# Low-rank product in four column groups, queries in two halves among the pieces of w_ada, rows turned by transposes, layers begun with half of the tokens, new instruction orders

## The reference, cut to what matters

```python
# block A, layers 0 and 1
shift, scale, gate = split(silu(c) @ w_ada + b_ada, 3)      # and the same for c_ctx
h  = x * (1 + scale) + shift;   hc = ctx * (1 + scale_c) + shift_c
# 16 projections of h and hc: q, k, v, gates, gla q, k, v, the low-rank pair g_af, g_ab
# (16 + 16 columns), sgu u, v, gate, and three merge gates
z = (pa @ a2 + ab)                                          # low rank, forward and backward
# attention (rope on x, keys of ctx and x), gated linear attention both ways, sgu
x_new = layer_norm(ALPHA * x + gate * (merge(...) @ w_out))
# block B, layers 0 and 1
h = rms_norm_2(x, norm_w);   proj = h @ w_in_2              # q, k, v, z_a, a, b, cf, z_b, gates
# depthwise conv, gated delta rule both ways, conv branch with layer norm, gated merge
x = x + y @ w_out
```

## Time and profile before

| | |
|---|---|
| Median of 3 runs | 1658.6 us (1658.0 to 1659.84) |
| The profiled execution, its own time | 1658.54 us |
| Its span, first to last instruction | 1656.7 us |
| TensorE busy with matmuls | 1590.9 us, 96% |
| TensorE weight loads | 1034.6 us, 62% |
| VectorE, ScalarE, GpSimd busy | 609.3, 412.7, 197.3 us |
| Moved by DMA | 183.64 MB, mean 111 GB/s |

### The profile page before, as it was taken

How to read it: one execution, slowest core, us unless ns; L and a number is a source line. 1 busy time by engine, 2 the same in 40 slices (tenths; PEclk the granted TensorE clock), 3 DMA queues, 4 the chain that set the end, 5 groups by cost and what they waited for, 6 DMA issues and landing times.

```text
span 1656.7 us, 18060 instructions
## 1 busy us (share of the span) xinstructions
PE 1590.9 (96%) x7424; PEld 1034.6 (62%) x7424; DVE 609.3 (37%) x1382; ACT 412.7 (25%) x786; POOL 197.3 (12%) x274
## 2 busy tenths in 40 slices
PE   4999999999999999999999999979999998999997
PEld 1544454455444444455686788558898757889883
DVE  1033343464100001523335312247577314667721
ACT  3114325422200000002234230032423203422220
POOL 0132100120010011112111102010100011010001
PEclk8999999999999999999999999989999998999999
DMA  9324332201221113222222234314313223331330
GB/s 389 154 102 154 119 119 93 101 29 48 76 76 77 76 51 132 91 107 102 102 102 102 102 135 170 142 56 154 129 72 126 99 98 147 126 129 54 125 127 39
DMA packets 16934, 183.64 MB, mean 111 GB/s; under 512 B 2258, under 2 KB 2642, under 8 KB 4564
## 3 DMA queue, kind: packets, MB, share of 16 engines
q1 hardware_dynamic: 16852, 182.49, 29.1%
HBM read 181.43 MB, written 1.05 MB: 110 GB/s over the span
## 4 chain that ended last, share of the span: by engine, by line
PE 93%; ACT 3%; DMA 2%; DVE 1%; POOL 0%; issue 0%; POOLq 0%; SPq 0%; ACTq 0%; DVEq 0%
PE ps L668 90%; PE ps L715 3%; DMA arena<-in_wf 2%; ACT arena L1162 1%; DVE arena L1551 1%; ACT L1505 0%; ACT L1503 0%; DVE arena L1548 0%; POOL arena L2094 0%; POOL arena L2098 0%; ACT arena L1503 0%; ACT arena L1394 0%; ACT L1396 0%; ACT L1394 0%; ACT arena L1378 0%
## 5 line engine op out<-in xcount | busy, mean ns | idle before, releaser
L668 PE MATMUL ps<-arena 128*128 128x256 f32 (+7 forms) x7036 | 1547.3, 404 | 33.6 <-DMA arena<-in_wf 17.9
L668 PEld LDWEIGHTS ps<-arena 128*128 128x128 f32 (+4 forms) x7036 | 988.5, 178 | 558.8 <-issue 435.5
L2094 POOL TENSOR_TENSOR arena<-arena 128x256 f32<-128x256 f32 (+4 forms) x214 | 162.8, 780 | 993.4 <-DVE arena L1551 588.5
L1551 DVE SCALAR_TENSOR_TENSOR arena<-arena 128x256 f32<-128x256 f32 (+3 forms) x443 | 211.2, 536 | 147.3 <-ACT arena L1267 41.1
L1162 ACT ACTIVATE arena<-ps 128x512 f32<-128x512 f32 (+4 forms) x252 | 131.8, 532 | 405.2 <-PE ps L668 382.1
L1551 DVE SCALAR_TENSOR_TENSOR arena<-arena,ps 128x256 f32<-128x256 f32 (+2 forms) x136 | 64.6, 482 | 391.7 <-PE ps L668 291.7
L1545 DVE TENSOR_TENSOR arena<-arena 128x512 f32<-128x512 f32 (+14 forms) x156 | 89.1, 593 | 127.4 <-ACT arena L1162 42.1
L715 PE MATMUL ps<-arena 128*128 128x128 f32 x384 | 62.5, 293 | 22.8 <-ACT arena L1162 18.2
L715 PEld LDWEIGHTS ps<-arena 128*128 128x128 f32 x384 | 47.4, 149 | 52.2 <-issue 27.1
L1333 ACT ACTIVATE arena<-ps 128x512 f32<-128x512 f32 (+1 forms) x24 | 13.5, 562 | 248.5 <-PE ps L668 248.5
L1548 DVE TENSOR_SCALAR arena<-arena 128x256 f32<-128x256 f32 (+9 forms) x181 | 64.7, 394 | 21.8 <-POOL arena L2094 17.0
(11 more groups left out here) (88 smaller groups left out, 305.1 us busy)
## 6 DMA issues: line engine op xcount, KB each, us to landing
arena<-in_wf SPq DMA_DIRECT2D x70, 2048.0 KB, 8.1
arena<-in_wf SPq DMA_DIRECT2D x20, 1024.0 KB, 6.9
arena<-in_wf SPq DMA_DIRECT2D x2, 1152.0 KB, 11.6
arena<-in_xinT SPq DMA_DIRECT2D x1, 2048.0 KB, 22.4
arena<-in_xin SPq DMA_DIRECT2D x4, 512.0 KB, 5.4
arena<-in_rp SPq DMA_DIRECT2D x2, 1024.0 KB, 10.7
arena<-in_consts SPq DMA_DIRECT2D x1, 1476.0 KB, 14.6
out<-arena SPq DMA_DIRECT2D x2, 512.0 KB, 2.6
```

Of the source, the lines that this page charges most:

```text
L668: return e.matmul(o, l, r, start=start, stop=stop, skip_group_check=True)
L1551: return e.scalar_tensor_tensor(out=o, in0=x, scalar=s, in1=y, op0=op0, op1=op1)
L2094: return e.tensor_tensor(o, x, y, op)
```

## The change

1. `ada_rows` copies the whole bank once, `ada_columns` makes four 128x128 transposes, and `ada_sum` first adds the four groups with a VectorE reduction into `AS`.
2. The piece of query weights of layer 0 is split in two halves over the inputs, `qa0` and `qa1`, which are fetched after the second and the fourth piece of w_ada. `hT` is made in two halves too, and the input `xT` comes in two transfers. `q_half(0, t)` accumulates inputs 0 to 511 of token tile t between the products of w_ada; `q_half(1, t)` adds the rest. The four query tiles have banks 2 to 5. The identity has a transfer of its own; the other constants, the biases of layer 1 and the parameters move behind `qa1` and `kv`.
3. "lr" is computed in four column groups, as the products of w_ada are; the z matmuls sum the four over 128 rows, with the low-rank weights repeated four times (`PZ`).
4. In layer A 1 the transposes of x become a dense step "hx" after the first two key-value products (context tokens); VectorE's part of `hT` moves with it.
5. In B, the first five products are made in two halves of 128 tokens (`half`), the first before the transposes of t = 1, in five banks (`HALF_BANKS`). The transposes of t = 0 of B 1 stand before the last output product of B 0, and GpSimd makes the power of B 0's t = 0 between its two of the last layer norm of A 1.
6. All four order strings are new.

The diff, cut to its core:

```diff
-PLAN = [(f"a{l}ada{j}", 4096) for l, j in ADA_FIRST] + plan_a(0) + plan_a(1) + plan_b(0) + plan_b(1)
+FIRST_PIECES = [x for n in range(2) for x in [(f"a{l}ada{j}", 4096) for l, j in ADA_FIRST[2 * n:2 * n + 2]] + [
+    (f"a0qa{n}", 2048)]]
+PLAN = FIRST_PIECES + plan_a(0) + plan_a(1) + plan_b(0) + plan_b(1)
...
-        steps = kv + [[("lr", 0, "A")] + ada(), []] + q + [ada()]
+        steps = kv[:2] + [[("hx", 0, "-")]] + kv[2:] + [[("lr", 0, "A")] + ada(), []] + q + [ada()]
...
-        FIRST = [("pf", 0, "A"), ("pf", 1, "A"), ("ps", 0, "V"), ("pf", 2, "A"), ("ps", 1, "V"), ("pf", 3, "A"),
-                 ("ps", 2, "V"), ("ps", 3, "V")]
+        FLAT = [[g for step in s for g in step if g[0] != "hx"] for s in DENSE]
+        FIRST = [("pf", 0, "A"), ("pf", 1, "A"), ("ps", 0, "V"), ("ps", 1, "V"), ("pf", 2, "A"), ("pf", 3, "A"),
...
+        HALF_BANKS = (0, 1, 6, 7, 5)
...
-                fetch(BADA[:, 24 * l:24 * l + 24], pa[l][:, 0:24], d_bada)
+            fetch(BADA[:, 0:24], pa[0][:, 0:24], d_bada)
+            fetch(cst[:, C_ID:C_MASK], consts[:, C_ID:C_MASK], d_id)
             load("a0ada2")
-            fetch(cst, consts[:, 0:C_W], d_cst)
-            load("a0ada1")
+            for n in range(2):
+                x = slice(2048 * n, 2048 * n + 2048)
+                fetch(arena[:, XT0:XT0 + 4096][:, x], xinT[:, x], d_xt[n])
+                load("a0ada3" if n == 0 else "a0qa1")
+            fetch(BADA[:, 24:48], pa[1][:, 0:24], d_bada)
+            fetch(cst[:, C_MASK:C_W], consts[:, C_MASK:C_W], d_cst)
+            load("a0kv")
             params(0)
-            load("a0ada3")
-            fetch(arena[:, XT0:XT0 + 4096], xinT, d_xt)
...
             def ada_columns(n, g, first):
-                p.wait_ge(landed(d_cst), dense_act(0, first, n))
+                p.wait_ge(landed(d_id), dense_act(0, first, n))
                 b = bank("dense", 0, g, n)
                 for i in range(4):
-                    ins = mm(b[:, 2 * i:2 * i + 2], PT4[n % 2][:, 128 * i:128 * i + 128], cst[:, C_STK:C_STK + 2],
-                             i == 0, True)
+                    ins = transpose(b, i, PT4[n % 2][:, 128 * i:128 * i + 128])
                 ins.then_inc(dn_pe.hit(0, GROUP[0][(g, n)]), 1)
+
+            def q_half(n, t):
+
+                w = use(f"a0qa{n}", 4)
+                b = psum("dense", 0, "q", t) if n else bank("dense", 0, "q", t)
+                for k in range(4):
+                    p.wait_ge(ht_made(0, 4 * n + k, t // 2))
+                    ins = mm(b, hT[:, 4 * n + k, 128 * t:128 * t + 128], w[:, k, :], n + k == 0, n + k == 4)
+                return ins
...
+            def input_turned(s):
+
+                for kp in range(4):
+                    b = bank("ht", s, kp)
+                    for i in range(4):
+                        kk, t = 2 * kp + i // 2, i % 2
+                        p.wait_ge(ln_x.at(0, 2 * s + t))
+                        ins = transpose(b, i, (X if s else CX)[:, 1024 * t + 128 * kk:1024 * t + 128 * kk + 128])
+                    ins.then_inc(ht_pe.hit(1, 4 * s + kp), 1)
...
-                            ins = feat(b, weights(f"a{l}kv", 8), 256, hT, 0, 512, [hk(l, k) for k in range(8)], 32)
+
+                            w = weights(f"a{l}kv", 8)
+                            for k in range(8):
+                                p.wait_ge(*hk(l, k))
+                                r = 32 * (k % 4)
+                                ins = mm(b[r:r + 32, :], w[:, k, 256:288], hT[:, k, :], k < 4, k >= 4)
...
-                        mm(bank("gla", l, "z", 2 * hp + d), PM[0:32, 256 * d + 128 * hp:256 * d + 128 * hp + 128],
-                           TH2[0:32, :], True, True).then_inc(gl_z.hit(l, 2 * hp + d), 1)
+                        mm(bank("gla", l, "z", 2 * hp + d), PZ[:, 256 * d + 128 * hp:256 * d + 128 * hp + 128],
+                           TH2, True, True).then_inc(gl_z.hit(l, 2 * hp + d), 1)
...
                         ada_products(n, "pf", *ADA_FIRST[n])
-                        if n:
-                            ada_columns(n - 1, "ps", "pf")
+                    for n in range(2):
+                        ada_columns(n, "ps", "pf")
+                    q_half(0, 0)
+                    q_half(0, 1)
+                    ada_products(2, "pf", *ADA_FIRST[2])
+                    q_half(0, 2)
+                    ada_products(3, "pf", *ADA_FIRST[3])
+                    ada_columns(2, "ps", "pf")
+                    q_half(0, 3).then_inc(dn_pe.hit(0, GROUP[0][("qh", 3)]), 1)
                     ada_columns(3, "ps", "pf")
                 else:
-                    for s in range(2):
-                        for kp in range(4):
-                            b = bank("ht", s, kp)
-                            for i in range(4):
-                                kk, t = 2 * kp + i // 2, i % 2
-                                p.wait_ge(ln_x.at(0, 2 * s + t))
-                                ins = transpose(b, i, (X if s else CX)[:, 1024 * t + 128 * kk:1024 * t + 128 * kk + 128])
-                            ins.then_inc(ht_pe.hit(1, 4 * s + kp), 1)
+                    input_turned(0)
...
             def dense_b(l):
-                made = made_b(l)
-                for n, c in DB:
-                    w = use(f"b{l}{n}", 8)
-                    ins = feat(bank("db", l, n, c), w, 128 * c, hB, 0, 256, made, 100 if n == "ab" else 128)
-                    ins.then_inc(db_pe.hit(l, GB_[(n, c)]), 1)
-                    yield
+                for i, (n, c) in enumerate(DB):
+                    if i < len(HALF_BANKS):
+                        ins = half(l, 1, n, c)
+                    else:
+                        ins = feat(bank("db", l, n, c), use(f"b{l}{n}", 8), 128 * c, hB, 0, 256)
+                    ins.then_inc(db_pe.hit(l, i), 1)
+                    yield
+
+            def half(l, t, n, c):
+
+                w = use(f"b{l}{n}", 8)
+                m = 100 if n == "ab" else 128
+                b = psum("db", l, n, c) if t else bank("db", l, n, c)
+                x = slice(128 * t, 128 * t + 128)
+                for k in range(8):
+                    p.wait_ge(hb_dve.at(l, 1 + k // 4) if t else hb_act.at(l, 3 + k // 4))
+                    ins = mm(b[0:m, x], w[:, k, 128 * c:128 * c + m], hB[:, k, x], t + k == 0, k == 7)
+                return ins
...
             def layer_b(l):
-                for t in range(2):
-                    for q in range(2):
...
+                if l == 0:
+                    input_b(0, 0)
+                for g in DB[:len(HALF_BANKS)]:
+                    half(l, 0, *g)
+                input_b(l, 1)
                 weave(ORDER_B[l], f=first_branch(l), c=conv(l), d=dense_b(l))
...
                     w = use(f"b{l}o{hf}", 8)
+                    if l == 0 and i == 3:
+                        input_b(1, 0)
...
-                b = psum("dense", 0, g, n)
-                for r in range(0, 128, 32):
-                    ins = copy(PT4[m % 2][r:r + 2, :], b[r:r + 2, :])
-                ins.then_inc(dn_act.hit(0, BY_ACT[0][(g, n)]), 1)
+                copy(PT4[m % 2], psum("dense", 0, g, n)).then_inc(dn_act.hit(0, BY_ACT[0][(g, n)]), 1)
...
+                e.tensor_reduce(AS.rearrange("p (a b) -> p a b", a=4), psum("dense", 0, g, n).rearrange(
+                    "p (i g r) -> p i r g", i=4, g=4)[:, :, 0:2, :], AX, ALU.add).then_inc(v.own(), 1)
...
+                        elif n == "hx":
+                            sc3 = r3(SCOL[1], 24)
+                            v.wait_ge(dense_dve(0, "es", 7))
+                            for kk in range(8):
+                                v.wait_ge(ht_pe.at(1, 4 + kk // 2))
+                                ts(hT[:, kk, 256:512], psum("ht", 1, kk // 2)[:, 256 * (kk % 2):256 * (kk % 2) + 256],
+                                   sc3[:, 8 + kk, 0:1], sc3[:, kk, 0:1], ALU.mult, ALU.add).then_inc(ht_dve.hit(1, kk), 1)
...
-                    g.wait_ge(at_red.at(l, t - 1) if t else None)
+                    g.wait_ge(at_red.at(l, t - 1) if t else ln_x.end(0) if l else None)
...
                     rstd(st6[:, 14:15], st6[:, 13:14]).then_inc(ln_rs.hit(l, k), 1)
+                    if l and k == 0:
+                        input_rstd(0, 0)
...
-        pa[l][0:16, PA_PM:PA_PM + 256] = I["gla_a2_f"][l]
-        pa[l][16:32, PA_PM + 256:PA_PM + 512] = I["gla_a2_b"][l]
+        for r in range(0, 128, 32):
+            pa[l][r:r + 16, PA_PZ:PA_PZ + 256] = I["gla_a2_f"][l]
+            pa[l][r + 16:r + 32, PA_PZ + 256:PA_PZ + 512] = I["gla_a2_b"][l]
```

More of the change, by code:

```diff
@@ L66, in plan_a @@
             out += [(f"a{l}b{b}{j}", 2048)]
-    return out + [(f"a{l}o{j}", 4096) for j in range(2)]
+    return (out if l else out[1:]) + [(f"a{l}o{j}", 4096) for j in range(2)]
 def plan_b(l):
@@ L198, in build_program @@
         cc, cs, st2 = fixed.take(16), fixed.take(16), fixed.take(4)
+        AS = fixed.take(8)
         SCOL = [fixed.take(48), fixed.take(48)]
@@ L527, in build_program @@
```

(4 more changed lines are left out.)

155 lines of the change are left out of this document (84 added, 71 removed).

## The result

The changed kernel takes 1593.35 us (median of 4 executions, 1588.55 to 1595.5) against 1658.51 us for the kernel before (1658.0 to 1659.84): ratio 0.960 (95% interval 0.958 to 0.963). The gain is 65 us; the forecast was 52.5, and its range ended at 1597. The profiled execution took 1595.5 us, its span 1593.7.

The account below looks back on a forecast made before the run. TensorE, busy for 96% of the span, was taken as the bound. Gains of 15.2, 4.4, 10.3, 7.4, 12.5 and 6.5 us sum to 56.3; 1658.5 less 56.3 plus 4 for shrunk cover gave 1606 us, range 1597 to 1621.

Parts of the forecast that it names:

- The start: Start to the end of layer 0's queries: half tiles among the w_ada products end at 54.8 instead of 70.0, gain 15.2 us.
- Rows turned by transposes: A 0's body: eight dense w_ada steps each save 0.55 us of TensorE time by four transposes, 4.4 us in all.
- Low rank: The "lr" product in both A layers: four column groups take 1.73 us instead of 6.86, gain 10.3 us, bounds 0 and 10.3.
- Rival 3: The column groups of "lr" don't run side by side: 10.3 us less gain, 1616 us, chance 0.04.
- z costs the same within 0.1 us: A's z matmuls: 128 rows instead of 32, same count and 512 columns, cost the same within 0.1 us each.
- Seams: Work put into TensorE's waits at the seams of A 1, B 0 and B 1 gains 7.4, 12.5 and 6.5 us.
- Rival 2: The clock falls at three seams and the queries' two starts: 7 us lost, 1613 us, chance 0.12.
- Cover that shrinks: A 0's attention chains and B have less TensorE work to hide behind: 4 us lost, bounds 0 and 17.
- The orders: The new order strings can spread the waits from shrunk cover; how well couldn't be read from a string, no separate gain priced.
- Rival 4: Cover is ample and old waits vanish with the new orders: 1600 us, chance 0.1.

Follow-up runs that it names:

- the three edits together: The changed kernel with four products in halves instead of five, the sixth product before the delta chain's first step, and 100 rows in the row matmuls: 1590.86 us.

## Why the prediction missed, step by step

- **The start**, 15.2 against 14.7: right in each time (begin, stall, end), and the run with late queries shows the cover to be real.
- **Rows turned by transposes**, 4.4 against 2.8. The steps are eight, as forecast, but 0.35 us each and not 0.55: columns and transposes are both followed by a change of mode. By starts a step takes 0.88 to 0.98 us before, and after 0.53 to 0.59 in seven and 0.88 in the one behind the low-rank product. I had priced the transposes by a pitch without that change.
- **Low rank**, 10.3: right, shown by its undoing. Rival 3 falls. The 7.5 us that I worked out from a factor of 2.38 should have been 8.0 (13.7 less 13.7 / 2.38); the factor measured is 3.8.
- **z costs the same within 0.1 us**: wrong in its ground, 1.3 us in all, measured alone. What I missed was not the rows but the change of mode around them.
- **Seams**, 7.4, 12.5 and 6.5 against 7.3, 12.8 and 5.9: right. Rival 2 falls, as the seams run at 1.00; its cost came 4 us behind them in B, at matmuls that the prediction never looked at. It is most of the -2.0 of B 0's body: 3.4 us lost there instead of 1.7.
- **Cover that shrinks, "I take 4"**: this step failed. Its reason, that the waits of A 0's body double (3.3 us more, and a little in B), didn't come true: 8 us of TensorE's work (5.1 and 2.8) went from there, and its idle time fell from 3.3 to 2.2 us. TensorE's waits from 76 us to the end of A 0's body, to be read against the earlier trace rows:

```profile
PE ps L688 <- ACT arena L1229: 1.4, 2, 0.7
PE ps L743 <- ACT arena L1229: 0.6, 1, 0.6
```

- **The orders had no price at all**, and this is the larger failed step. I wrote that they "can spread this" and stopped. They take 32 of the 39 changes of mode out, 6.4 us in A's bodies at 0.2, and the other edits' gains at the seams hang on them: 28 us with all four strings.

A's bodies then add up: 10.3 for low rank, 2.8 for the rows, 39 changes x 0.2 = 7.8 (an estimate, by the price measured), 1.5 less idle time, 22.4 of 22.8 us measured. The forecast had 14.6, less 4. Rival 4 (1600, old waits vanish) had the right sign and too small a cause: of what it describes only 1.5 us came. A price for the change of mode was to be had from the trace of before, where a record of 512 columns lasts 522 ns ahead of one and 429 elsewhere; what can't be read there beforehand is how many the new strings would leave, except by counting them through the strings.

What stays open: whether it is the 36 rows or their mode that brings the clock down, and why single executions of a kernel differ in it. The late stretch of the three edits together isn't theirs alone: the second profile of the changed kernel has half clock for 3.4 us at 1246.8 and at 1523.3 us, where its first has none, and the kernel before has it at 1300.1 and 1583.4. Nothing here says what brings it. The 0.4 us left in A's bodies is not assigned.

## What to carry to other kernels

Before pricing an edit of TensorE's work, list the tiling modes in the order of issue: a lone matmul of another mode costs two changes, and an order that groups them gains without taking any work away. Price an order together with the edits that need it: here it was worth about 6 us alone and 28 with them. And after closing the waits at a seam, look at the granted clock of the 20 us behind it, for a few matmuls there can give back part of what was won: here 3.4 us behind each seam of B, of 12.8 and 5.9 won.

## What the hardware showed that I had not expected

- A change of tiling mode: 0.20 us, 93 ns on the record ahead and 104 ns on the record behind (55 where that is a transpose).
- 32 rows are as fast as 128 inside a mode: 429 ns a record of 512 columns.
- Transposes and 128-column products, 20 us of them on end with waits under 1 us, ran at granted clock 1.00; the clock fell behind them, at matmuls of 36 rows, in 22 of 22 profiled seams, and in none of six with 100 rows. Behind whole products and 36 rows it fell in some profiles and not in others.
- Eight matmuls in four column groups: 1.85 us against 6.98, 3.8 times.
